# Two neighbouring weight k-tiles woven together in SBUF, ring slots 128 bytes further apart

## What is computed

```python
xn = rmsnorm(x, mix_norm_g[l])
p = xn @ w_in[l]                                   # 1024 -> sum of SPLITS
(aq, ak, av, ao, ai, af, bb, bc, bx, cz, cxbc, cdt, sq, sk, sv, gates) = jnp.split(p, SPLIT_POINTS, axis=-1)
ya = mlstm(...)                                    # matrix memory
yb = short_conv_mixer(bb, bc, bx, b_conv_w[l])
yc = mamba2_mixer(...)
yd = stick_breaking_attention(sq, sk, sv)
lifted = jnp.einsum('bsie,ied->bsid', ycat, w_lift[l])
merged = jnp.einsum('bsid,bsid->bsd', g, lifted)   # g = sigmoid(gates)
x = x + merged @ w_out[l]
x = x + conv_glu_mlp(rmsnorm(x, ffn_norm_g[l]), w_up[l], ffn_conv_w[l], ffn_conv_b[l], w_down[l])
return rmsnorm(x, final_norm_g)
```

## Time and profile before

| | |
|---|---|
| median of two runs | 1038.17 us (1037.79 to 1038.56) |
| the profiled execution | 1038.42 us, its span 1036.7 us, mean granted TensorE clock 0.992 |
| instructions in the span | 12635, of them 4724 matmuls and 4724 weight loads |
| DMA | 108.24 MB, mean 104 GB/s |

### The profile page before, as it was taken

The page is one execution under the profiler, slowest core; times in us unless marked ns, Lnnn a source line. Parts: engine busy times, 40 slices in busy tenths (PEclk is TensorE's granted clock), DMA queues, the critical chain, the costliest instruction groups (busy, mean ns, idle before and its releaser), DMA issues.

```text
span 1036.7 us, 12635 instructions
## 1 busy us (share of the span) xinstructions
PE 1019.0 (98%) x4724; PEld 837.8 (81%) x4724; DVE 593.2 (57%) x764; ACT 424.3 (41%) x515; POOL 67.6 (7%) x74
## 2 busy tenths in 40 slices
PE   8999999999999999999999999989999999999996
PEld 7897888887777887777888888868888888888886
DVE  6835754656676566556364456687656666543323
ACT  5514445644435322444432333544444344332331
POOL 5610000000000000000000000320000000000002
PEclk9999999999999999999999999989999999999998
DMA  6332222223222333343252222513233222253312
GB/s 238 114 113 70 82 84 82 77 93 105 89 85 82 120 122 124 132 132 103 81 183 87 97 88 97 181 61 119 85 100 101 100 86 88 68 176 94 102 56 81
DMA packets 32024, 108.24 MB, mean 104 GB/s; under 512 B 3684, under 2 KB 5860, under 8 KB 31600
## 3 DMA queue, kind: packets, MB, share of 16 engines
q1 hardware_dynamic: 29520, 93.86, 27.1%
q0 software_dynamic: 2320, 13.69, 4.0%
q10 hardware_dynamic: 144, 0.14, 0.1%
HBM read 103.42 MB, written 4.25 MB: 104 GB/s over the span
## 4 chain that ended last, share of the span: by engine, by line
PE 93%; DVE 4%; ACT 2%; issue 1%; DMA 1%; DVEq 0%; SPq 0%; ACTq 0%
PE gb L413 81%; PE gb L446 4%; DVE w_lo L985 1%; PE xb L596 1%; PE gb L524 1%; PE xb L556 1%; PE xb L549 1%; PE xb L536 1%; PE xb L413 1%; ACT w_hi L701 1%; PE xb L513 1%; DMA raw<-w_stream 1%; DVE y_lo L993 1%; PE gb L464 1%; PE xb L584 0%
## 5 line engine op out<-in xcount | busy, mean ns | idle before, releaser
L985 DVE TENSOR_TENSOR w_lo<-raw,w_hi 128x1024 fp32r<-128x1024 f32 (+2 forms) x181 | 218.1, 1206 | 342.8 <-ACT w_hi L701 342.4
L701 ACT ACTIVATE w_hi<-raw 128x1024 fp32r<-128x1024 f32 (+2 forms) x181 | 183.8, 1017 | 413.5 <-PE gb L413 380.8
L413 PE MATMUL gb<-xn_hi,w_hi 128*128 128x512 f32 x720 | 285.0, 396 | 0.0
L413 PE MATMUL gb<-xn_hi,w_lo 128*128 128x512 f32 x720 | 281.1, 390 | 0.0
L413 PE MATMUL gb<-xn_lo,w_hi 128*128 128x512 f32 x720 | 281.0, 390 | 0.0
L413 PE MATMUL gb<-y_hi,w_hi 128*128 128x512 f32 x400 | 159.1, 398 | 6.0 <-DVE y_lo L993 4.2
L413 PEld LDWEIGHTS gb<-xn_hi,w_hi 128*128 128x128 f32 x720 | 135.8, 189 | 29.7 <-issue 1.0
L413 PEld LDWEIGHTS gb<-xn_lo,w_hi 128*128 128x128 f32 x720 | 135.8, 189 | 29.0 <-issue 1.4
L413 PEld LDWEIGHTS gb<-xn_hi,w_lo 128*128 128x128 f32 x720 | 135.6, 188 | 28.6
L413 PE MATMUL gb<-y_lo,w_hi 128*128 128x512 f32 x400 | 156.6, 391 | 0.0
L413 PE MATMUL gb<-y_hi,w_lo 128*128 128x512 f32 x400 | 156.4, 391 | 0.0
(11 more groups left out here) (231 smaller groups left out, 1018.4 us busy)
## 6 DMA issues: line engine op xcount, KB each, us to landing
raw<-w_stream SPq DMA_DIRECT2D x149, 512.0 KB, 3.3
raw<-w_down SPq DMA_DIRECT2D x16, 384.0 KB, 3.0
abc<-scr_a POOLq DMA_DIRECT2D x8, 640.0 KB, 4.1
raw<-w_down SPq DMA_DIRECT2D x16, 320.0 KB, 2.8
x_in<-xT SPq DMA_DIRECT2D x8, 256.0 KB, 6.5
x<-xT POOLq DMA_DIRECT2D x1, 2048.0 KB, 8.5
scr_x<-x POOLq DMA_DIRECT2D x1, 2048.0 KB, 7.4
x<-scr_x POOLq DMA_DIRECT2D x1, 2048.0 KB, 8.4
```

The source lines that it names most:

```text
L413: ins = pe.matmul(out, w[:, r, lo:hi], rhs(k)[x], start=(first and n == 0 and q == 0), stop=(last_ and n == len(ks) - 1 and q == 2))
L701: act.activation(w_hi[:, r, 0:n], raw[:, r, 0:n], ACT.Copy).then_inc(S["hi_ready"], 1)
L985: dve.tensor_tensor(w_lo[:, r, 0:n], raw[:, r, 0:n], w_hi[:, r, 0:n].bitcast(F32), ALU.subtract)\
```

## The change

A load now reads every second float. The host weaves the columns of two neighbouring k-tiles (column 0 of the first, column 0 of the second, column 1 of the first, and so on), so that k-tile kk of a slot starts at float (kk // 2) * 256 + kk % 2 and has a step of 2 floats, 8 bytes. This holds for every unit but those of the value projections. The slots of w_hi and w_lo lie 4096 + 128 bytes apart, and what stands behind them moves up by 1024 bytes in all; all other tiles keep their distances. A down tile's units hold 6, 6, 6 and 4 k-tiles, since a pair cannot be cut. Number and sizes of the matmuls and loads, and all semaphores, stay.

```diff
+STEP = 32
-DOWN_K = [6, 6, 5, 5]
-DOWN_K0 = [0, 6, 12, 17]
+DOWN_K = [6, 6, 6, 4]
+DOWN_K0 = [0, 6, 12, 18]
+LANES = 2
...
-    w_hi = m.put("w_hi", [P, RING, 1024], F32R)
-    w_lo = m.put("w_lo", [P, RING, 1024], F32R)
+    w_hi = m.put("w_hi", [P, RING, 1024 + STEP], F32R)[:, :, 0:1024]
+    m.at = base + (m.at - base + LINE - 1) // LINE * LINE
+    w_lo = m.put("w_lo", [P, RING, 1024 + STEP], F32R)[:, :, 0:1024]
+    m.at = base + (m.at - base + LINE - 1) // LINE * LINE
...
-        def gemm(out, r, c0, rhs, ks, kk0=0, kstep=1, first=True, last_=True):
+        def ktile(w, r, kk, lanes=LANES, n=P):
+
+            c0 = kk // lanes * lanes * P + kk % lanes
+            return w[:, r, c0:c0 + lanes * (n - 1) + 1:lanes]
+
+        def gemm(out, r, kk, rhs, ks, first=True, last_=True, lanes=LANES):
...
-                lo, hi = c0 + n * P, c0 + n * P + P
                 for q, (w, x) in enumerate(((w_hi, 0), (w_hi, 1), (w_lo, 0))):
-                    ins = pe.matmul(out, w[:, r, lo:hi], rhs(k)[x], start=(first and n == 0 and q == 0),
+                    ins = pe.matmul(out, ktile(w, r, kk + n, lanes), rhs(k)[x], start=(first and n == 0 and q == 0),
...
-                        ins = pe.matmul(gb(o)[0:96, :], w[:, u % RING, P * k:P * k + 96], xn(k)[x],
+                        ins = pe.matmul(gb(o)[0:96, :], ktile(w, u % RING, k, n=96), xn(k)[x],
...
+    def lanes(w, n=LANES):
+
+        k, c = w.shape
+        w = w.reshape(k // (P * n), n, P, c).transpose(2, 0, 3, 1)
+        return np.ascontiguousarray(w).reshape(P, -1)
```

More of the change, by code:

```diff
@@ L153, in build @@
     raw = m.put("raw", [P, RING, 1024])
-    w_hi = m.put("w_hi", [P, RING, 1024], F32R)
-    w_lo = m.put("w_lo", [P, RING, 1024], F32R)
+    w_hi = m.put("w_hi", [P, RING, 1024 + STEP], F32R)[:, :, 0:1024]
+    m.at = base + (m.at - base + LINE - 1) // LINE * LINE
+    w_lo = m.put("w_lo", [P, RING, 1024 + STEP], F32R)[:, :, 0:1024]
+    m.at = base + (m.at - base + LINE - 1) // LINE * LINE
+    X0 = m.at
     xn_hi = m.put("xn_hi", [P, KD, T], F32R)
@@ L237, in build @@
     assert G0 + 4 * T * (8 + 2) <= A0 and A0 + 4 * T * KD <= C0
-    x2 = at("x2", [P, KD, T], F32, base + 3 * RING * 4096)
+    x2 = at("x2", [P, KD, T], F32, X0)
     GB = [ctx.enter_context(nc.psum_tensor(f"gb{i}", [P, T], F32)) for i in range(4)]
@@ L459, in unit @@
                 for q in range(2):
-                    ins = gemm(gb(o + q)[:, :], u % RING, q * T, yk, range(4))
+                    ins = gemm(gb(o + q)[:, :], u % RING, 4 * q, yk, range(4))
             elif u == U_SMALL:
@@ L479, in _ @@
                     pe.wait_ge(S["lo_ready"], u + 1)
-                ins = gemm(GB[u][:, :], u, k * P, xg, [k], first=(k == 0), last_=(k == KD - 1))
+                ins = gemm(GB[u][:, :], u, k, xg, [k], first=(k == 0), last_=(k == KD - 1))
         ins.then_inc(S["unit_done"], 2)
@@ L610, in _ @@
                     pe.wait_ge(S["merged_ready"], k + 1)
-                ins = gemm(gb(first_tile[u])[:, :], u % RING, k * P, mg, [k], first=(k == 0), last_=(k == KD - 1))
+                ins = gemm(gb(first_tile[u])[:, :], u % RING, k, mg, [k], first=(k == 0), last_=(k == KD - 1))
             ins.then_inc(S["unit_done"], 1)
@@ L624, in _ @@
                         pe.matmul(X[0][:, :], ones[:], f_ac[:], start=True, stop=True).then_inc(S["n2_sum"], 1)
-                ins = gemm(gb(first_tile[u])[:, :], u % RING, k * P, x1g, [k], first=(k == 0), last_=(k == KD - 1))
+                ins = gemm(gb(first_tile[u])[:, :], u % RING, k, x1g, [k], first=(k == 0), last_=(k == KD - 1))
             ins.then_inc(S["unit_done"], 1)
@@ L635, in _ @@
                         pe.wait_ge(S["n2_ready"], k + 1)
-                    ins = gemm(GB[(TILES0 + BANK0 + q) % 4][:, :], (U_UP + q) % RING, k * P, mg, [k], first=(k == 0),
+                    ins = gemm(GB[(TILES0 + BANK0 + q) % 4][:, :], (U_UP + q) % RING, k, mg, [k], first=(k == 0),
                                last_=(k == KD - 1))
@@ L1413, in lay_out @@
     stream = np.zeros((N_STREAM, P, 1024), np.float32)
+    def lanes(w, n=LANES):
+        k, c = w.shape
+        w = w.reshape(k // (P * n), n, P, c).transpose(2, 0, 3, 1)
+        return np.ascontiguousarray(w).reshape(P, -1)
     def put(u, w, width=P):
         for n in range(w.shape[1] // width):
-            stream[u + n] = slabs(w[:, n * width:(n + 1) * width])
+            stream[u + n] = lanes(w[:, n * width:(n + 1) * width])
     def put_tokens(u, w):
@@ L1426, in lay_out @@
     small[:, 0:4], small[:, 32:36], small[:, 64:72] = ai, af, cdt
-    stream[U_SMALL] = slabs(small)
+    stream[U_SMALL] = lanes(small)
     put(U_AQ, aq); put(U_AK, ak); put_tokens(U_AV, av); put(U_AO, ao)
@@ L1431, in lay_out @@
         for q, w in enumerate((bc, bx, bb)):
-            stream[U_B + 3 * n + q] = slabs(w[:, n * P:n * P + P])
+            stream[U_B + 3 * n + q] = lanes(w[:, n * P:n * P + P])
     lift = f["w_lift"][0]
@@ L1437, in lay_out @@
                 d0 = P * (2 * t + q)
-                stream[u0 + 3 * t + q] = slabs(gt[:, D * b + d0:D * b + d0 + P])
-                stream[u0 + 3 * t + 2, :, 512 * q:512 * q + 512] = slabs(lift[b][:, d0:d0 + P])
+                stream[u0 + 3 * t + q] = lanes(gt[:, D * b + d0:D * b + d0 + P])
+                stream[u0 + 3 * t + 2, :, 512 * q:512 * q + 512] = lanes(lift[b][:, d0:d0 + P])
     put(U_OUT, f["w_out"][0])
@@ L1443, in lay_out @@
         for q in range(2):
-            stream[U_UP + 2 * t + q] = slabs(up[:, FF * q + P * t:FF * q + P * t + P])
+            stream[U_UP + 2 * t + q] = lanes(up[:, FF * q + P * t:FF * q + P * t + P])
     down = np.zeros((4 * KD, P, 6 * P), np.float32)
@@ L1449, in lay_out @@
             k0, n = DOWN_K0[q], DOWN_K[q]
-            down[4 * t + q, :, 0:n * P] = slabs(wd[k0 * P:(k0 + n) * P, t * P:t * P + P])
+            down[4 * t + q, :, 0:n * P] = lanes(wd[k0 * P:(k0 + n) * P, t * P:t * P + P])
     def cols(v):
```

## The result

The changed kernel took 1058.36 us (1057.85 to 1058.86, two runs) against 1038.17 us, a ratio of 1.0194 (95% interval 1.0151 to 1.0238). The forecast was 1001 us, a gain; the change costs 20 us. The range reached up to 1060 us and so took the time in, but that is luck: its upper part was there for rivals A and C, and neither of them is what happened.

What follows compares the result with a forecast made beforehand. The prediction took the spacing of TensorE's matmuls, not its waits, to bound the kernel. A 39.2 us saving less 2.0 given back left 37.2 off 1038.2, so 1001.0 us; range 988 to 1060 us.

Steps and rivals of the forecast that it cites:

- A: Rival: nothing changes, the 13.3 ns are a fixed price of a load under a full-rate stream; 1038 us, chance 0.14 (with gains under 2%).
- C: Rival: the load itself takes twice as long, showing under 132 matmuls of 256 columns; 13 us more, 1051 us, chance 0.06.
- Part 1: L413 and L464 matmuls: with loads stepping 8 bytes the loss was taken as 3.3 ns, saving 39.2 us in all.
- the plain-float row: Profile row of L556, eight plain-float matmuls in 2.16 us, 3.3 ns lost each; nearest row with load and stream at one pace.
- the cold stretch: Ten L413 starts at granted clock 0.50, after PE idled 4.16 us: 0.427 us each, no loss, stream and load at unequal pace.
- rival B: Slower: the stream loses in proportion to what the load walks, 26.7 ns a matmul; 52 us more, 1090 us, chance 0.20.
- Part 3: Slots 4224 bytes apart in place of 4096: L446's 384 matmuls could gain or lose up to 5 us; taken as 0.
- Parts 2 and 4: L446 keeps its weight layout: 0. DVE, ACT and SP work as before, down tiles split 6, 6, 6, 4 under busy PE: no cost.
- Part 5: Given back: 1.0 us more waiting for y_lo before the second norm, 1 us for w_lo and attention-stage waits; 2.0 us in all.

Runs made afterwards that it cites:

- The bursts: Separate programs, only loads and mostly 72 matmuls per burst on an idle core, varying weight place, step, columns and type; contiguous float32r loads at place 0 took 0.2267 us each.

## Why the prediction was wrong

**What bounds the kernel** was right: the spacing of L413's matmuls, not a wait. The whole difference is in it.

**Part 1, the step: the step that failed.** "I take 3.3 ns: at one pace the two readers keep their distance, so after a first meeting they need not meet again." The loss of a float32r matmul of 512 columns with step 2 is 20.0 ns at place 0 and between 16.7 and 22.2 at the places tried. In place of a saving of 10.0 ns there is a cost of 6.7 at place 0, and of 6.2 on the mean of the changed kernel's long piece. The value came from the plain-float row, in which two things differed from L413: the ratio of the paces and the rate of the stream. The bursts hold them apart: plain float loses 2.5 ns with steps of 1, 2 and 4 alike, though only step 1 is at one pace, and float32r at one pace loses 20. The prediction had the counterexample in hand: in the cold stretch the paces were unequal and nothing was lost. It gave that to rival B as a remark and did not lower the forecast for it.

**Part 3, the slots: mis-sized.** Taken as 0 for L413; it was asked only for L446, where it is worth 0.1 us. For the contiguous loads the 128 bytes cost 3.3 ns a matmul, 11.2 us in all. For the woven ones they give 0.4 ns back (0.2329 against 0.2333 for even slots; the bursts at places 0, 128, 256 and 384 average 0.2330), 2 us. The guess behind it, that the loss may depend on the distance from a multiple of 512 bytes, was right in kind; the period is 256 for contiguous loads.

**Parts 2 and 4** held: the value projections moved by 0.12 us, and the split alone by -0.1 us. **Part 5** held as a mechanism, with the sign of part 1: 96 matmuls that are 6.2 ns slower should take 0.6 us off the wait for y_lo, and it shrank by 0.5. The further 1 us for other waits did not show: the waits listed for PE add up to 9.8 us before and 9.4 after.

**The rivals.** A (a fixed price) is out, since place changes it. C (a load twice as slow) put the kernel at 1051 us, the nearest of the times, but its price is not there: the 256-column matmuls kept 0.120 us, and a load that slow came only with step 4. B was on the right side too. Its mechanism, a loss in proportion to what the load walks, is wrong (one column loses 17.8 ns) and its 26.7 ns were too much; the measured 19.6 ns lie just beyond the 18.6 from which it was to decide. Its true part is what it said of the cold stretch: a loss above 3 ns was seen only where the moving operand is read over 9.6 bytes of a partition a ns. In bfloat16 and plain float (4.8 bytes a ns) it is 2.5 ns, in the cold stretch none. One burst gave a moving operand a step of two floats; its 512 columns took 0.451 us, 24 ns above the 0.427 of half rate, and no run here takes that apart.

**What stays open.** Why a load disturbs a full-rate stream at all, down to one column, and why the spacings settle into repeating patterns, some of them two for the same instructions. Nothing here shows the inside of that.

## What to carry to other kernels

When a stretch of matmuls is bound by its own spacing, compare the spacing with columns divided by the clock: in float32r the rest (6% here) depends in these runs on where stationary and moving tiles lie relative to each other, so keep their starts a multiple of 256 bytes apart and the stationary columns together, and measure each other layout in a burst of 72 matmuls before putting it into a kernel. A comparison row must differ from the case in one thing only; plain float differed from float32r in the rate of the stream and in the ratio of the paces, and the wrong one was given the credit.

## What was not expected of the hardware

- The place of a weight tile relative to the moving tile changes the spacing of float32r matmuls between 0.2267 and 0.2342 us, with a period of 256 bytes for contiguous loads. Moving only 8 bytes away costs 4 ns (16.61 us for 72) and 4 bytes 5.7 ns (16.73), while 16 bytes to either side cost nothing (16.33 at place 16, 16.32 at 240).
- Loading 1 column costs the stream more (17.8 ns) than loading 128 (13.3 ns).
- In bfloat16 (0.2158 to 0.2161 us) neither steps of 2 and 4 nor a place of 32 bytes made a difference, and in plain float (0.4292 us for each of the two instructions of a matmul) no step did; its place was not varied.
- Two burst states for the same instructions, 0.2300 and 0.2333 us, by what ran ahead; the kernel in such a place lay 5 us apart over four runs. In the changed kernel slots 0 and 2 swap their 0.233 and 0.235 us across the second norm.
